# Four feed-forward blocks in seven half-width products per 2x2 set of tiles, with the conditioning rows moved ahead of them

## Chip, cores and metric

One core of one Trainium2 chip. The metric is the device time of one launch in microseconds (us). The profile is of one execution on the chip.

## What is computed

The reference runs two transformer blocks over 512 tokens of width 1024 in fp32. What matters here (cut):

```python
def _conv_ffn(h, w_up, conv_w, w_down):
    u = causal_depthwise_conv(h @ w_up, conv_w)
    a, b = jnp.split(u, 2, axis=-1)
    return (jax.nn.silu(a) * b) @ w_down

def swiglu(h, w_gu, w_down):
    g, u = jnp.split(h @ w_gu, 2, axis=-1)
    return (jax.nn.silu(g) * u) @ w_down

c_act = jax.nn.silu(c)
for i in range(2):
    mod = c_act @ mod_w[i] + mod_b[i]          # 9 vectors of 1024: shift, scale, gate, three times
    sh0, sc0, g0, sh1, sc1, g1, sh2, sc2, g2 = jnp.split(mod, 9, axis=-1)
    x = x + 0.5 * g0 * swiglu(modulate(rms_norm(x, norm_g[i, 0]), sh0, sc0), ffn_w_gu[i, 0], ffn_w_down[i, 0])
    x = x + g1 * mixer(modulate(rms_norm(x, norm_g[i, 1]), sh1, sc1))   # pooling, then differential attention
    x = x + 0.5 * g2 * swiglu(modulate(rms_norm(x, norm_g[i, 2]), sh2, sc2), ffn_w_gu[i, 1], ffn_w_down[i, 1])
```

`_conv_ffn` stands once, in the block ahead of this loop, and `swiglu` four times. Each has 1024 inputs, 2 x 2816 hidden columns and 1024 outputs.

## The kernel before

Activations lie transposed, features on the 128 partitions and 512 tokens along the free axis. A product in fp32 is made of three in the rounded type fp32r: a value is split into a high part (rounded) and a low part (the rest), and `product` (L1924 to L1926) issues high weight by high activation, high by low, and low by high, each 128x128 by 512 columns, into one PSUM bank. A weight unit is one output tile of 128 features: SP loads it into one of the four slots of `stage`, ACT writes its high part (`hi`, L655), DVE its low part (`lo`, L1144), each into one of two buffers, and PE waits for DVE.

The program runs in this order: the input products of the first mixer (`mix_in`), its merge and its output product (`mix_out`), feed-forward block 0 with the convolution (`up0`, `down0`), block 1, the pooling mixer, blocks 2 and 3, the attention, and block 4. Ahead of each stands a normalisation, in which PE spreads the scale over the partitions (`spread_rstd`, L1960), ACT and DVE round and split the normalised rows, and POOL makes half of the low parts (L564). In a feed-forward block `up` takes 44 units of 24 matmuls (22 pairs of a gate tile and an up tile) and `down` 8 outputs of 22 hidden tiles each, in three units; the pairs run in a loop of two. Of each pair ACT takes the silu of the gate (L715), DVE the product (L1234), and ACT and DVE split it (L718, L1241). In block 0 DVE also applies the taps of the convolution (L1216 to L1221).

The 144 conditioning rows (`mod`, L1185) are on DVE: each multiplies a 512 KB slice of `mod_w` by the activated condition and sums it. Slices come by POOL's queue (L536) into two buffers. 25 stand in `mix_in`, 32 in the merge, 7 in `mix_out`, 21 in `down0`, 44 in `up1` and 15 in `down1`.

Each engine runs its own list in the order in which the program is written; what holds an instruction back is the semaphores named at its wait. The change touches `plan_stream`, the loading on SP, `mod_loads` on POOL, and `up`, `down` and `mod` on each engine.

## Time and profile before

| | us |
|---|---|
| median of 3 runs | 2854.73 (2853.56 to 2866.36) |
| span of the profiled execution | 2868.0 |
| PE, ACT, DVE, POOL busy in it | 2783.2, 979.6, 1428.6, 241.9 |
| from one normalisation's spread to the next, feed-forward block 2 | 369.6 |
| the same, feed-forward block 3 | 369.1 |

The span is the profiled execution's own time, from its first instruction to its last. PE is busy in 97% of it. A row of a timeline begins with the start and the length; in brackets stand the idle time of that engine before the row and what ended it. PE rows overlap (a matmul's record is longer than the distance to the next), so the pace of PE is read from one start to another.

### The profile page before, as it was taken

The page shows a single profiled execution, that of the slowest core. Times are in us where ns is not written, and L with a number is a line of the kernel's source. Part 1 is how long each engine was busy: PE and PEld are TensorE (multiplying, and loading weights), DVE is VectorE, ACT ScalarE, POOL GpSimd, SP SyncE. Part 2 cuts the span into 40 slices and gives each one's busy share as a digit, 9 for nine tenths or more (in the row PEclk, how much of TensorE's full clock was granted, in tenths as well). Part 3 has the DMA queues.
Part 4 walks back from the last instruction along what each step waited for, and adds up shares of the span by engine and source line. Part 5 has one row for each costly group of instructions (what it writes and reads, how often), then busy time and mean ns, then how long its engine had stood idle before and what let it go on. Part 6 is the DMA issues. An engine that isn't in the chain of part 4 may idle for free.

```text
span 2868.0 us, 40754 instructions
## 1 busy us (share of the span) xinstructions
PE 2783.2 (97%) x16211; PEld 2249.2 (78%) x16211; DVE 1428.6 (50%) x2059; ACT 979.6 (34%) x1530; POOL 241.9 (8%) x318
## 2 busy tenths in 40 slices
PE   8999888999999999999989999999999999999998
PEld 7855777887887878888878888788887866788887
DVE  4588643666776455555443332433324876433322
ACT  3355443333332232222342222322223265422222
POOL 1000110112000111001110000100002300100000
PEclk8899999999999999999999999999999999999999
DMA  6331001673332655566323333233333310233332
GB/s 234 115 99 59 3 3 32 218 229 118 102 93 87 204 152 195 186 199 197 100 68 95 95 95 98 88 95 95 92 101 97 108 37 23 77 100 95 93 94 70
DMA packets 89844, 311.07 MB, mean 108 GB/s; under 512 B 11632, under 2 KB 12400, under 8 KB 89584
## 3 DMA queue, kind: packets, MB, share of 16 engines
q1 hardware_dynamic: 66928, 232.62, 26.0%
q0 software_dynamic: 22784, 76.56, 8.7%
q8 instruction: 98, 1.61, 0.2%
q14 instruction: 34, 0.28, 0.0%
HBM read 305.99 MB, written 2.10 MB: 107 GB/s over the span
## 4 chain that ended last, share of the span: by engine, by line
PE 91%; DVE 4%; ACT 3%; issue 1%; POOL 1%; DMA 1%; SPq 0%; DVEq 0%; ACTq 0%; POOLq 0%
PE psum L1924 24%; PE psum L1926 24%; PE psum L1925 24%; PE psum L2101 1%; PE psum L2103 1%; PE psum L2102 1%; PE psum L2612 1%; PE psum L2601 1%; PE psum L1999 1%; PE psum L1995 1%; PE psum L1996 1%; PE psum L2303 1%; PE psum L2076 1%; PE psum L2392 1%; PE psum L2273 1%
## 5 line engine op out<-in xcount | busy, mean ns | idle before, releaser
L1144 DVE TENSOR_TENSOR w_lo<-stage,w_hi 128x1024 fp32r<-128x1024 f32 (+2 forms) x441 | 518.3, 1175 | 827.4 <-ACT w_hi L655 827.2
L655 ACT ACTIVATE w_hi<-stage 128x1024 fp32r<-128x1024 f32 (+2 forms) x441 | 449.7, 1020 | 1206.1 <-PE psum L1926 1171.7
L1924 PE MATMUL psum<-h_hi,w_hi 128*128 128x512 f32 (+1 forms) x2024 | 792.7, 392 | 3.3 <-DVE w_lo L1144 2.3
L1925 PE MATMUL psum<-h_lo,w_hi 128*128 128x512 f32 (+1 forms) x2024 | 790.9, 391 | 0.0
L1926 PE MATMUL psum<-h_hi,w_lo 128*128 128x512 f32 (+1 forms) x2024 | 790.5, 391 | 0.0
L1924 PEld LDWEIGHTS psum<-h_hi,w_hi 128*128 128x128 f32 (+1 forms) x2024 | 381.1, 188 | 86.7 <-DVE w_lo L1144 4.4
L1926 PEld LDWEIGHTS psum<-h_hi,w_lo 128*128 128x128 f32 (+1 forms) x2024 | 381.0, 188 | 80.2
L1925 PEld LDWEIGHTS psum<-h_lo,w_hi 128*128 128x128 f32 (+1 forms) x2024 | 381.1, 188 | 79.6
L1924 PE MATMUL psum<-hid_hi,w_hi 128*128 128x512 f32 x880 | 344.0, 391 | 6.5 <-DVE hid L1234 6.5
L1926 PE MATMUL psum<-hid_hi,w_lo 128*128 128x512 f32 x880 | 343.4, 390 | 0.0
L1925 PE MATMUL psum<-hid_lo,w_hi 128*128 128x512 f32 x880 | 343.2, 390 | 0.0
L1924 PEld LDWEIGHTS psum<-hid_hi,w_hi 128*128 128x128 f32 x880 | 165.7, 188 | 42.9 <-DVE hid L1234 8.6
L1234 DVE TENSOR_TENSOR hid<-s_buf,psum 128x512 f32<-128x512 f32 x88 | 60.5, 687 | 266.5 <-PE psum L1926 264.9
L1926 PEld LDWEIGHTS psum<-hid_hi,w_lo 128*128 128x128 f32 x880 | 165.6, 188 | 34.5
L1925 PEld LDWEIGHTS psum<-hid_lo,w_hi 128*128 128x128 f32 x880 | 165.7, 188 | 34.2
L1185 DVE CUSTOM_DVE_ANT_0 mod_w<-mod_w,c_act 128x1024 f32<-128x1024 f32 x144 | 175.3, 1217 | 0.1
L536 POOL DMA_DIRECT2D mod_w<-in_mod_w x144 | 76.9, 534 | 1036.5 <-DVE modv L1185 859.2
L718 ACT ACTIVATE hid_hi<-hid 128x512 f32 (+1 forms) x110 | 68.0, 618 | 54.8 <-DVE hid L1234 54.8
L666 ACT ACTIVATE norm_t<-xT 128x512 f32<-128x512 f32 x64 | 40.2, 630 | 128.2 <-DVE xT L1258 121.2
L557 POOL TENSOR_TENSOR rexp<-norm_t 128x512 f32<-128x512 f32 x8 | 10.3, 1286 | 820.5 <-ACT norm_t L666 820.5
L1241 DVE TENSOR_TENSOR hid_lo<-hid,hid_hi 128x512 f32 (+1 forms) x110 | 75.2, 683 | 0.0
L557 POOL TENSOR_TENSOR rexp<-rexp,norm_t 128x512 f32<-128x512 f32 x40 | 51.4, 1285 | 270.5 <-ACT norm_t L666 269.9
(440 smaller groups left out, 3023.0 us busy)
## 6 DMA issues: line engine op xcount, KB each, us to landing
stage<-in_up SPq DMA_DIRECT2D x220, 512.0 KB, 3.6
mod_w<-in_mod_w POOLq DMA_DIRECT2D x144, 512.0 KB, 4.3
stage<-in_down SPq DMA_DIRECT2D x80, 448.0 KB, 3.3
stage<-in_down SPq DMA_DIRECT2D x40, 512.0 KB, 3.5
stage<-in_w_in SPq DMA_DIRECT2D x24, 512.0 KB, 3.6
stage<-in_w_qkv SPq DMA_DIRECT2D x24, 512.0 KB, 3.6
stage<-in_w_merge SPq DMA_DIRECT2D x16, 512.0 KB, 4.5
turned_n<-in_cmp_w SPq DMA_DIRECT2D x1, 4096.0 KB, 13.1
```

What stands on the lines that cost most here:

```text
L536: pool.dma_start(mod_w[:, slot], A["mod_w"][bass.ds(t, 1)].rearrange("a p n -> (a p) n")).then_inc(mod_in[slot], 16)
L557: pool.tensor_tensor(sq_sum, sq(n_norm, 0) if k == 1 else sq_sum, sq(n_norm, k), ALU.add).then_inc(acc_done, 1)
L655: act.activation(w_hi[:, c % 2, 0:kt * cols], stage[:, c % NSTAGE, 0:kt * cols], ACT.Copy).then_inc(hi_done, 1)
L666: act.activation(sq(n_norm, k), xT[:, k], ACT.Square).then_inc(sq_done, 1)
L718: act.activation(hid_hi[:, bass.ds(2 * i + q, 1), :].rearrange("p a n -> p (a n)"), hid[:, q], ACT.Copy).then_inc(hidhi_done, 1)
L1144: dve.tensor_tensor(w_lo[:, c % 2, 0:kt * cols], stage[:, c % NSTAGE, 0:kt * cols], w_hi[:, c % 2, 0:kt * cols].bitcast(F32), ALU.subtract ...
L1185: dve.tensor_tensor_reduce(out=mod_w[:, t % 2], in0=mod_w[:, t % 2], in1=c_act[:], scale=1.0, scalar=0.0, op0=ALU.mult, op1=ALU.add, accum ...
L1234: dve.tensor_tensor(hid[:, q], s_buf[:, q], taps[:, 1] if f == 0 else bank(s.tile + 2 * q + 1), ALU.mult).then_inc(hid_done, 1)
L1241: dve.tensor_tensor(hid_lo[:, tile, :].rearrange("p a n -> p (a n)"), hid[:, q], hid_hi[:, tile, :].rearrange("p a n -> p (a n)").bitcast( ...
L1924: pe.matmul(dst, wh[:, n], a_hi[:, k], start=start and n == 0, stop=False)
L1925: pe.matmul(dst, wh[:, n], a_lo[:, k], start=False, stop=False)
L1926: m = pe.matmul(dst, wl[:, n], a_hi[:, k], start=False, stop=stop and n == kt - 1)
```

## The change

**Feed-forward blocks 1 to 4.** The first four units (two gate tiles, two up tiles) stay as they were (`first_units` and two more, with 512 columns). All else is taken in sets of two by two: two output tiles, input tiles in pairs, and two halves of the tokens. Such a set, called a group, is made of seven products `P1` to `P7` of half width (256 columns) in place of eight. Ten groups `g` (two gate tiles each) alternate with ten groups `u` (two up tiles each); each takes the place of two units, has four pairs of inputs, and 12 matmuls in a product. For the outputs the pairs of hidden tiles are taken in two rounds of four, with four groups `d` (two output tiles each) in a round, and the last three pairs in six groups of one to three (`CLOSING`): 34 groups with 124 pairs in all, listed in `GROUPS`.

The products need sums and differences of weights and of activations. Five parts of weights are split for each group: `a` and `b` (1024 wide, two pieces each), `s4`, `s2` and `q` (512 wide). Three of the weight sums are made by DMAs that add into SBUF, issued by POOL (`sum_s1`, `sum_s3`, `sum_s4`), one on DVE (`sum_s2`). The split buffers are single: a part of the next group is written when the product that read the last one is done. The sums of the normalised rows are made on POOL (`hsum`), their differences on DVE. Products come together in PSUM: ACT copies intermediate states out (`snap`), DVE adds (`row1`, `c22`), and PE goes on in the same bank once a copy was made. Hidden pieces are kept in seven forms (the four quarters but one, and four combinations), which ACT and DVE split as 1792 columns at once.

PE runs `P1` and `P5` of a group, then `P3` of the one before, `P6`, `P4` of the one before, `P2` and `P7`.

**Conditioning rows.** All 144 stand ahead of block 1: 25 in `mix_in`, 40 in the merge, 14 in `mix_out`, 22 in `up0` (one a pair) and 43 in `down0`. The two buffers of `mod_w` and that of the condition then serve blocks 1 to 4.

The diff, cut:

```diff
+HALF = S // 2
+ROUNDS = [(0, 4), (4, 4)]
+CLOSING = [(8, 2, 1), (8, 2, 3), (8, 3, 0), (10, 1, 1), (8, 3, 2), (10, 1, 3)]
...
+ST_PE = in_turn(["P1", "P5", "P3", "P6", "P4", "P2", "P7"], ("P3", "P4"), ["P3", "P4"])
+ST_SPLIT = in_turn(["a", "s4", "s2", "q", "b"], ("s4", "q"), ["s4", "q"])
+PART_OF = {"P1": "a", "P5": "a", "P3": "s4", "P6": "s2", "P4": "q", "P2": "b", "P7": "b"}
...
-        MOD_AT = {"mix_in": 0, "merge": 25, "mix_out": 57, "down0": 64, "up1": 85, "down1": 129}
+        MOD_AT = {"mix_in": 0, "merge": 25, "mix_out": 65, "up0": 79, "down0": 101}
...
+            def sum_s1(f, G):
+                n, q = group_kp(G) * P, place[f, G, 0]
+                pool.wait_ge(loaded[q % NSTAGE], 16 * (q // NSTAGE + 1))
+                pool.dma_start(stage[:, q % NSTAGE, n:2 * n], group_source(f, G)[:, 4 * n:5 * n],
+                               accum_op=ALU.add).then_inc(st_s1_in[G % 2], 16)
...
+                for G in range(NG + 1):                      # ACT, per group
...
+                            snap("s1", G)
+                            snap("s5", G)
+                            part_hi("a", G + 1)
...
+                        silu("12", G - 1)
+                        part_hi("s4", G)
+                        snap("s6", G)
+                        part_hi("s2", G + 1)
...
+                        part_hi("q", G)
+                    if late == "u":
+                        hid_high(late_at)
+                        part_hi("b", G + 1)
+                    if kind == "g":
+                        silu("22", G)
...
                         lo(c + 2, i)
...
-                        if f == 1:
-                            mod(MOD_AT["up1"] + 2 * q, i)
+                        mod(MOD_AT["up0"] + q, i)
                         lo(c + 3, i)
...
-                        if s.name in MOD_AT and n < KD - 1:
-                            mod(MOD_AT[s.name] + 3 * n + j)
+                        if n < KD - 1:
+                            for t in range(43 * (3 * n + j) // 21, 43 * (3 * n + j + 1) // 21):
+                                mod(MOD_AT[s.name] + t)
...
+                for G in range(NG + 1):                      # DVE, per group
...
+                        sum_s2(G + 1)
+                        part_lo("a", G + 1)
+                        row1(G - 1)
...
+                        hid_dif(late_at)
+                        part_lo("s4", G)
...
+                        part_lo("s2", G + 1)
+                        hid21(G - 1)
+                        hid_dif4(late_at)
...
+                        part_lo("q", G)
+                        part_lo("b", G + 1)
+                    if late == "u":
+                        hid_low(late_at)
+                        c22(G)
...
+                def strassen(name, G):                       # PE
+                    kp = group_kp(G)
+                    pe.wait_ge(st_lo, split_of(f, PART_OF[name], G))
+                    bank_free(name, G)
...
+                    dst = gamma(G) if name in ("P5", "P3") else alpha(G) if name == "P2" else beta(G)
+                    start, stop = name in ("P1", "P5"), name in ("P4", "P3")
+                    for j in range(kp):
+                        w, low = wh[:, j * P:(j + 1) * P], wl[:, j * P:(j + 1) * P]
+                        pe.matmul(dst, w, operand(name, G, 0, j), start=start and j == 0, stop=False, skip_group_check=True)
+                        pe.matmul(dst, w, operand(name, G, 1, j), start=False, stop=False, skip_group_check=True)
+                        m = pe.matmul(dst, low, operand(name, G, 0, j), start=False, stop=stop and j == kp - 1,
+                                      skip_group_check=True)
+                    m.then_inc(st_prod, 1)
```

In `bank_free`, `P6` waits for the copy `s1` of its group, `P2` for `s5`, `P7` for `s6`, and `P4` for `c22`; `P1` and `P5` wait until the group two back has been taken out of their banks.

**Where instructions stand.** DVE at the start of the up part of block 1 before: the last low part of the normalised rows, then two units (`w_lo<-stage,w_hi` is the low part of a weight unit):

```order
L1172 SCALAR_TENSOR_TENSOR h_lo<-rexp,modv,h_hi 128x512 [waits hhi_done]
L1144 TENSOR_TENSOR w_lo<-stage,w_hi 128x1024 [waits hi_done]
L1234 TENSOR_TENSOR hid<-s_buf,psum 128x512 [waits unit_done,silu_done]
L1144 TENSOR_TENSOR w_lo<-stage,w_hi 128x1024 [waits hi_done]
L1241 TENSOR_TENSOR hid_lo<-hid,hid_hi 128x512 [waits hidhi_done]
```

and DVE after the change, while PE is at a gate group `g`. The rows are the low part of `a`, `row1` and the product of the pair before (L1728), the differences of its hidden pieces (L1760, L1763), low parts of `s4` and `s2`, the fourth quarter and its difference (L1751, L1771), low parts of `q` and `b`, the low part of the seven hidden pieces (L1777), and `c22` of `g` (L1735):

```order
L1672 TENSOR_TENSOR w_lo<-stage,w_hi 128x1024 [waits st_hi]
L1721 TENSOR_TENSOR c_act<-psum,c_act 128x512 [waits st_snap,st_prod]
L1728 TENSOR_TENSOR hraw<-c_act,rexp 128x512 [waits st_hlo,st_silu,st_row1]
L1760 TENSOR_TENSOR hraw<-hraw 128x512 [waits st_mult]
L1763 SCALAR_TENSOR_TENSOR hraw<-hraw 128x256 [waits st_ht]
L1672 TENSOR_TENSOR w_lo<-mod_w,w_hi 128x512 [waits st_hi] x2
L1751 SCALAR_TENSOR_TENSOR hraw<-psum,rexp 128x256 [waits st_silu,st_prod]
L1771 SCALAR_TENSOR_TENSOR hraw<-hraw 128x256 [waits st_hid21,st_ht]
L1672 TENSOR_TENSOR w_lo<-mod_w,w_hi 128x512 [waits st_hi]
L1672 TENSOR_TENSOR w_lo<-stage,w_hi 128x1024 [waits st_hi]
L1777 TENSOR_TENSOR hid_lo<-hraw,hid_hi 128x1792 [waits st_hhi]
L1735 TENSOR_TENSOR norm_t<-psum,norm_t 128x256 [waits st_snap,st_prod]
```

Where four instructions stood for two units, thirteen now stand for a group, which takes the place of two units. The matching rows of ACT after the change, from the high part of `a` on; the last but two is a silu, and the last two are the copies `s1` and `s5` of the up group `u`:

```order
L1027 ACTIVATE w_hi<-stage 128x1024 [waits st_prod,st_s1_in1,loaded3]
L1027 ACTIVATE w_hi<-mod_w 128x512 [waits st_prod,st_s4_in0]
L1040 ACTIVATE norm_t<-psum 128x256 [waits st_prod]
L1027 ACTIVATE w_hi<-mod_w 128x512 [waits st_prod,st_s2]
L1027 ACTIVATE w_hi<-mod_w 128x512 [waits st_prod,st_a22_0]
L1061 ACTIVATE hid_hi<-hraw 128x1792 [waits st_ht]
L1027 ACTIVATE w_hi<-stage 128x1024 [waits st_prod,st_s3_in1,loaded0]
L1054 ACTIVATE norm_t<-norm_t 128x256 [waits st_c22]
L1040 ACTIVATE c_act<-psum 128x256 [waits st_prod,st_mult]
L1040 ACTIVATE c_act<-psum 128x256 [waits st_prod]
```

The copy `s1` of `u` stands behind the silu (L1054), which waits for DVE's `c22`, the last row of the fence before. Third, DVE in `up0` after the change; the rows of L1576 are new there, and before, L1626 was followed at once by the low part of the next unit:

```order
L1626 TENSOR_TENSOR hid<-s_buf,taps 128x512 [waits unit_done,silu_done,tap_done]
L1576 ISA mod_w,modv<-mod_w,c_act 128x1024 [waits mod_in1]
L1576 ISA modv 128x1
L1535 TENSOR_TENSOR w_lo<-stage,w_hi 128x1024 [waits hi_done]
L1632 TENSOR_TENSOR hid_lo<-hid,hid_hi 128x512 [waits hidhi_done]
```

A conditioning row now stands between the product of a pair and the low part of a unit, which PE waits for.

## Rows read from the trace of the kernel before

**Rows 1.** The page's busy times, shares and instruction counts by engine.

```profile
PE 2783.2 (97%) x16211; PEld 2249.2 (78%) x16211; DVE 1428.6 (50%) x2059; ACT 979.6 (34%) x1530; POOL 241.9 (8%) x318
```

**Rows 2.** Windows, block 2: length, busy PE, PEld, DVE, ACT, POOL; clock, DMA, GB/s.

```profile
1455.00:1824.00 369.00, 367.22 (x1622) 303.40 (x1621) 124.09 (x136) 107.70 (x136) 12.90 (x10) 1.00 0.31 93
```

**Rows 3.** Chain of waits, the spreads at both ends of block 2: start, length, what.

```profile
1455.02 1.72 PE psum L1960 x8
...
1824.65 1.17 PE psum L1960 x8
```

**Rows 4.** Timeline of PE in `up2`, first matmuls of units four apart.

```profile
1498.95 0.39 PE L1924 MATMUL psum<-h_hi,w_hi 128*128 128x512 f32 x1
...
1520.71 0.39 PE L1924 MATMUL psum<-h_hi,w_hi 128*128 128x512 f32 x1
```

**Rows 5.** Timeline of PE in the pooling mixer, 256-column matmuls 27 apart.

```profile
1424.68 0.28 PE L2526 MATMUL psum<-w_hi,h_hi 128*128 128x256 f32 x1
...
1427.90 0.28 PE L2526 MATMUL psum<-w_hi,h_hi 128*128 128x256 f32 x1
```

**Rows 6.** DVE by line and shape: busy, mean ns, idle before and its releaser.

```profile
L1144 DVE TENSOR_TENSOR w_lo<-stage,w_hi 128x1024 fp32r<-128x1024 f32 x340 | 416.1, 1224 | 528.3 <-ACT w_hi L655 528.2
...
L1241 DVE TENSOR_TENSOR hid_lo<-hid,hid_hi 128x512 f32 x90 | 61.5, 683 | 0.0
...
L1612 DVE TENSOR_TENSOR psum<-psum,tri 128x256 f32<-128x256 f32 x32 | 13.8, 430 | 18.6 <-PE psum L2303 18.5
```

**Rows 7.** ACT by line and shape, same columns.

```profile
L655 ACT ACTIVATE w_hi<-stage 128x1024 fp32r<-128x1024 f32 x340 | 360.7, 1061 | 967.5 <-PE psum L1926 934.6 <-PE psum L1999 27.6 <-PE psum L2496 2.0
...
L655 ACT ACTIVATE w_hi<-stage 128x512 fp32r<-128x512 f32 x20 | 12.5, 625 | 9.5 <-PE psum L1926 7.9 <-PE psum L2528 1.6
...
L970 ACT ACTIVATE X<-psum 128x256 f32<-128x256 f32 x40 | 15.2, 381 | 37.9 <-PE psum L2390 32.9 <-PE psum L2368 3.9
```

**Rows 8.** Timeline of ACT in `up2`, released by a unit's last matmul.

```profile
1499.15 1.06 ACT L655 ACTIVATE w_hi<-stage 128x1024 fp32r<-128x1024 f32 x1 [3.86 <-PE psum L1926]
```

**Rows 9.** Timeline of DVE in `up2`, two instructions that follow each other.

```profile
1505.69 1.23 DVE L1144 TENSOR_TENSOR w_lo<-stage,w_hi 128x1024 fp32r<-128x1024 f32 x1 [0.34 <-ACT w_hi L655]
1506.83 0.68 DVE L1241 TENSOR_TENSOR hid_lo<-hid,hid_hi 128x512 f32 x1
```

**Rows 10.** Timeline of PE, first matmuls after two short stops.

```profile
1420.95 0.40 PE L2526 MATMUL psum<-w_hi,h_hi 128*128 128x256 f32 x1 [2.62 <-POOL h_lo L564]
...
2445.19 0.80 PE L1924 MATMUL psum<-h_hi,w_hi 128*128 128x512 f32 x1 [1.78 <-DVE w_lo L1144]
```

**Rows 11.** Windows right behind those stops (columns of rows 2).

```profile
1421.00:1424.40 3.40, 3.40 (x17) 3.40 (x18) 3.10 (x5) 2.64 (x4) 1.52 (x2) 0.52 0.00 0
...
2445.00:2448.00 3.00, 2.81 (x7) 2.26 (x8) 1.36 (x3) 1.58 (x2) 0.00 (x0) 0.52 0.57 156
```

**Rows 12.** Timeline of POOL, the last low part ahead of block 2.

```profile
1466.52 1.29 POOL L564 TENSOR_TENSOR h_lo<-rexp,h_hi 128x512 fp32r<-128x512 f32 x1 [0.90 <-ACT h_hi L699]
```

**Rows 13.** The page's costliest groups, an addition of two 128x512 tiles on POOL.

```profile
L557 POOL TENSOR_TENSOR rexp<-rexp,norm_t 128x512 f32<-128x512 f32 x40 | 51.4, 1285 | 270.5 <-ACT norm_t L666 269.9
```

**Rows 14.** Timeline of DVE in `up0`, second taps of a pair and the next unit's low part.

```profile
766.25 0.75 DVE L1216 TENSOR_SCALAR taps<-psum,vec 128x512 f32<-128x512 f32 x1 [0.81 <-PE psum L1926]
...
769.59 1.22 DVE L1144 TENSOR_TENSOR w_lo<-stage,w_hi 128x1024 fp32r<-128x1024 f32 x1
```

**Rows 15.** Chain of waits in the merge, a conditioning row, its buffer's next load, the next row.

```profile
621.18 1.22 DVE mod_w L1185
...
623.05 5.08 DMA mod_w<-in_mod_w
628.16 1.22 DVE mod_w L1185
```

**Rows 16.** The page's DMA queues: packets, MB, share of 16 engines' span.

```profile
q1 hardware_dynamic: 66928, 232.62, 26.0%
```

**Rows 17.** The page's DMA issues: KB each, median us from issue to landing.

```profile
mod_w<-in_mod_w POOLq DMA_DIRECT2D x144, 512.0 KB, 4.3
```

713 lines of the change are left out of this document (603 added, 110 removed).

## Prediction

> **What bounds the kernel now.** I read the page's busy times first: PE is busy in 2783.2 of 2868.0 us [rows 1]. Then the windows, to see whether that holds where the change works: in feed-forward block 2 PE is busy in 367.2 of 369.0 us at full clock, DVE in 124.1 and ACT in 107.7 [rows 2]. The chain of waits dates the block from one spread to the next, 1455.02 to 1824.65, 369.6 us [rows 3]. Blocks 1 to 4 are alike. So a block's time is its matmuls: four units of 24 take 1498.95 to 1520.71, 21.76 us for 96, or 0.2267 us each [rows 4]. ACT and DVE idle for two thirds of a block; the reader should see that this slack is an average, and that a unit's weights are split a whole unit ahead.
>
> The profiled execution, 2868.0 us, is 13.3 us longer than the median of runs, 2854.73. The sum is made against 2868.0; I take 13 off at the end. What a measurement can tell from no change is about 0.5%, 14 us.
>
> **Matmuls: a gain.** Per block 62 units with 1488 matmuls of 512 columns go, 337.3 us at 0.2267. In their place come 124 pairs x 7 x 3 = 2604 of 256 columns. The nearest rows are the pooling mixer's fp32r matmuls of 256 columns, each with a weight load of its own as here: 27 steps in 3.22 us, 0.1193 us each [rows 5]. That makes 310.7 us, **26.7 us less** per block, 107 in four. A product of 12 is 1.43 us, a group 10.02, a pair of groups (g, u) 20.04 where 21.76 was.
>
> The Trainium skill's page "TensorE: Matmul & The Clock Gate" (section on the back-to-back issue gap) would give N/2.4 + 2.5 ns, 216 and 109 ns; by it a block saves 36.6 us, all four 40 us more, and the forecast would be about 2996. The rows [rows 4, 5] show 10 ns more per matmul at both widths, and I keep the rows.
>
> **A pair of groups: a new wait.** The question is whether ACT and DVE, which run their lists in order, follow PE in 20 us. Their durations: a split of 1024 columns takes 1.22 on DVE and 1.06 on ACT, of 512 0.68 and 0.63, a PSUM operation of 256 columns 0.43 and 0.38 [rows 6, 7]. The 1792-column split has no row; by the slope from 512 to 1024 columns (1.06 ns a column on DVE, 0.85 on ACT) I estimate 2.03 and 1.71, nearest to the 1024 row; the ends are two 1024-splits (2.45, 2.12) and the slope alone (1.9, 1.5). ACT starts 0.20 after the last matmul it waits for (1499.15 after 1498.95) [rows 4, 8]; instructions on one engine overlap by 0.09 (1.23 long, 1.14 apart) [rows 9].
>
> From P1 of g at 0, as the order fences list it. ACT copies s1 at 1.63 and s5 at 3.07, and splits `a` for u, 3.36 to 4.42. DVE takes `a` low to 5.68, row1 to 6.28, the product of the pair before to 7.0, its two differences to 8.17, s4 and s2 low to 9.35, the last quarter and its difference to 10.15, q low to 10.74. ACT meanwhile can split the seven hidden pieces only when the last difference is there: 10.18 to 11.90. Behind it stands `b` for u, to 12.86. DVE: `b` low to 14.12, the low part of the hidden pieces to 16.06, c22 of g to 16.40. ACT: the silu on c22 to 16.84, then the copy s1 of u, 16.75 to 17.13. PE's P6 of u waits for that copy. It is due after one group and three products, at 14.3, and starts at 17.2: **PE idles 2.8 us**, once in each pair. All links are data or queue order between ACT and DVE; none shortens because an average is low. The u half has slack: DVE holds 6.7 us of work there, 10.8 in the g half. P7 of u loses 0.4 more behind the copy s6, so the pair takes 23.25 us at full clock.
>
> The clock comes on top. After idling 2.62 us PE was granted 0.52 of full clock (near its lower level of 1.2 GHz, of 2.4) for the next 3.4 us, and after 1.78 us 0.52 for 3.0 us [rows 10, 11]. A stop of 2.8 us lies above both. At half clock 3.3 us do the work of 1.7; the loss is partly taken from the wait that follows, and the walk gives **24.45 us**, 4.4 more than PE's work. Nine pairs of a block meet the wait: 39.6 us. Bounds: no stop, 0; and 6 us a pair, if the 1792-column splits cost like two of 1024 and the cross-engine waits 0.1 more each.
>
> **Start of a block.** The four plain units stay. The normalised rows' sums are new on POOL: the last low part there ends at 1467.81, 12.8 after the spread [rows 3, 12], then come eight additions of 128x512 at 1.285 [rows 13]. Seven end at +21.8, a little later for two DMA issues ahead of them; DVE's difference and the low part of the fourth unit follow to 25.5, where PE wanted it at 22.3. So 3.2 us. The first `a` comes 1.7 late, and P6 of the first group 5.7, since the split of the first hidden pieces stands on ACT ahead of the first copy. 10.6 us, with two more for the clock: **12.6**. Bounds 5 and 18.
>
> **Closing groups.** Products of 3 to 9 matmuls give 30.1 us of PE work, but the splits and the additions to x keep DVE 31 to 37 us: **8** us, bounds 0 and 14. The eight full groups for outputs keep PE's pace: each has 7 DVE splits and sums and 6 additions, about 8.5 us of 10.
>
> **Per block** -26.7 + 39.6 + 12.6 + 8 = **+33.5**, in four **+134**.
>
> **Conditioning rows.** Removed from block 1, where PE hid them: nothing gained. New places: `up0`, one in each pair ahead of the next unit's low part. There DVE's second taps begin at 766.25, and that low part ends at 770.81 [rows 14]; the unit's slot is at 766.05 + 5.44 = 771.49, slack 0.68 us. A row costs 1.14, so PE stops 0.5 per pair: with 0.1 for restarts, 22 x 0.6 = **13** us. In `down0` 43 rows stand in 21 slots of about 4.99 us (22 matmuls). With two buffers, a row, the issue, the load and the row again take 621.18 to 628.16, 6.98 us for two rows [rows 15]; with the median load of 4.3 instead of 5.08 [rows 17], 6.2 to 6.4. 21 x 1.4 = **28** us (13 to 41). In the merge and `mix_out` fifteen rows more: **6** (0 to 13). Together **+47**, bounds 25 and 70; a slot that gives PE a stop of a microsecond can also cost clock, which is the upper end.
>
> **Bytes.** A block reads 124 x 8 blocks of 65.5 KB, 65.0 MB where it read 32.5; 24.4 MB of it are added into SBUF. The queue of loads moved 232.6 MB in 26.0% of the span, 312 GB/s while busy [rows 16], so a block has 130 us of plain transfers and 78 more if an adding transfer costs the same. No row has one; bounds are 1 times a plain one (it moves no less) and 3 times (a read of the source, a read and a write of the destination), 208 to 365 us of about 400. I take it as hidden.
>
> **Sum.** 134 + 47 = +181: 3049 against 2868.0, **3036** against the median. The range of this case: 2985 to 3085, by the bounds on the wait and the rows.
>
> **Rivals.**
> 1. Lighter stops (0.22). The clock stays up after 2.8 us: nine pairs lose 3.2 each, start and closing 15.6, so a block -26.7 + 28.8 + 15.6 = +17.7, four 71 us; rows at their lower bound, 25: **2951**. For it: ACT's real waits could be shorter by a few handoffs, and stops then stay under those of rows 10. Against it: [rows 11] shows both short stops followed by half clock.
> 2. PE stays the bound (0.14), and the kernel is **faster**. Decides: the chain from P1 of g to the copy of u must fit. Of its 17.2 us the part after q low is the 1792-split, `b`, hidden low, c22 and silu; with PE due at 14.34 it must lose 2.8 us, a fifth of the 14 us in which DVE and ACT work. Then -107, with 20 for starts and closings and 25 for rows: **2793**. For it: 50% idle ACT and DVE. Against: each duration is a row, and the order is fixed.
> 3. Adding transfers bind (0.10). At three times a plain one a block's transfers take 365 us, and some 50 pass at its start and end in which only the four slots can be filled ahead; `s1`, `s3`, `s4` land late: a landing of more than about 8 us (4.3 for a 512 KB load) stops the split of `a`, thus P1. A block then takes some 415 us, four 182 more, with 47 for rows **3084**. By the Trainium skill's "DMA: Bandwidth & Descriptors" (rules for kernel authors) an accumulating DMA reads its destination and writes it later; that speaks for more than the plain price, and no run here shows how much.
> 4. Gain and stops cancel (0.09), within 0.5%: stops of 1 us a pair and 10 us at start and end, so a block -7.7, against 31 for the rows: about **2855**, 2840 to 2869.
>
> My forecast has 0.45. The range of 2850 to 3110 leaves out most of rival 2 and the upper tail of 3, less than 0.2. Faster 0.14 (rival 2), same 0.09 (rival 4), slower 0.77 (forecast and rivals 1 and 3).
>
> **What to look for.** Busy PE falls from 97% to under 90%. The three lines of 256-column matmuls run at 0.119 us. PE idles 2.5 to 3 us ahead of P6 of each u, released by ACT's copy of s1, with a granted clock near 0.5 behind it; a pair of groups takes 24.4 us, a block about 403. In `up0` and `down0` PE waits for DVE's low parts. DMA bytes rise by 130 MB to about 440. I am wrong if P6 starts without idling (rival 2), if the stops leave the clock at 1.0 (rival 1), or if DMA waits lead the idle time (rival 3).

## The result, and the profile after

The changed kernel takes 3222.95 us (median of 4 runs, 3216.45 to 3227.45), the kernel before in the same session 2854.14: a ratio of 1.128 with a 95% interval of 1.124 to 1.131. It is slower, as forecast, but by 369 us, not by 181, and it lies outside the range of 2850 to 3110. The profiled execution spans 3220.5 us, 352.5 more than the one before (2868.0).

The page's first part after the change (for before: [rows 1]):

```profile
PE 2826.8 (88%) x20675; PEld 2483.1 (77%) x20675; DVE 2140.2 (66%) x3253; ACT 1318.6 (41%) x2206; POOL 639.8 (20%) x758
```

The windows from one normalisation's spread to the next: block 0, then blocks 1 to 4 (columns as in [rows 2]).

```profile
691.10:1121.00 429.90, 391.65 (x1624) 310.12 (x1623) 298.51 (x420) 111.51 (x134) 46.40 (x73) 0.96 0.47 157
1121.00:1554.40 433.40, 366.38 (x2737) 354.55 (x2738) 299.03 (x433) 191.81 (x306) 112.25 (x120) 0.92 0.67 156
...
1594.50:2037.50 443.00, 374.95 (x2739) 362.84 (x2739) 299.51 (x431) 194.03 (x307) 112.30 (x120) 0.90 0.66 153
2037.50:2478.10 440.60, 369.68 (x2739) 357.69 (x2738) 299.60 (x432) 193.42 (x306) 112.25 (x120) 0.91 0.66 154
...
2769.70:3202.20 432.50, 365.76 (x2738) 353.19 (x2738) 297.08 (x430) 191.78 (x304) 112.23 (x120) 0.92 0.65 150
```

The spread ahead of block 0 came at 673.0 before and at 691.1 now, and block 0 took 373.3 us before: the stages with moved rows lost 18.1 + 56.6 = 74.7 us. Blocks 1 to 4 took 368.9, 370.1, 369.1 and 368.8 before; they lost 64.5, 72.9, 71.5 and 63.7, together 272.6. The other stages make up the last 5. The reader should see the clock in the window rows: PE's busy time in blocks 1 to 4, 367 to 368 us before, is 366 to 375 us now, although a block's matmuls are 27 us less at full clock. At 0.90 to 0.92 of the clock they take longer.

**Where PE stops in block 2.** The timeline of PE, with the idle time ahead of a row and what ended it:

```profile
1620.77 0.80 PE L2520 MATMUL psum<-h_hi,w_hi 128*128 128x512 f32 x1 [8.64 <-DVE w_lo L1535]
...
1678.82 0.36 PE L2670 MATMUL psum<-dif_hi,w_hi 128*128 128x256 f32 x1 [3.02 <-issue]
...
1702.01 0.55 PE L2670 MATMUL psum<-dif_hi,w_hi 128*128 128x256 f32 x1 [3.00 <-issue]
...
1726.67 0.55 PE L2670 MATMUL psum<-hid_hi,w_hi 128*128 128x256 f32 x1 [6.20 <-DVE hid_lo L1777]
...
1797.75 0.55 PE L2670 MATMUL psum<-dif_hi,w_hi 128*128 128x256 f32 x1 [3.00 <-issue]
...
1823.36 0.36 PE L2670 MATMUL psum<-dif_hi,w_hi 128*128 128x256 f32 x1 [3.00 <-issue]
...
1847.81 0.35 PE L2670 MATMUL psum<-dif_hi,w_hi 128*128 128x256 f32 x1 [3.02 <-issue]
...
1989.42 0.55 PE L2670 MATMUL psum<-hid_hi,w_hi 128*128 128x256 f32 x1 [3.88 <-issue]
...
2031.85 0.80 PE L2535 MATMUL psum<-cst,rexp 128*128 128x1 f32 x3 [4.99 <-POOL rexp L779]
```

The stops of 3.0 us are those ahead of P6 that the prediction walked to (2.8); "issue" only says that the view finds no releaser for a wait on ACT's copies. What ended it is seen on DVE and on ACT just ahead of 1702.01:

```profile
1698.84 2.02 DVE L1777 TENSOR_TENSOR hid_lo<-hraw,hid_hi 128x1792 fp32r<-128x1792 f32 x1
1700.77 0.42 DVE L1735 TENSOR_TENSOR rexp<-psum,rexp 128x256 f32<-128x256 f32 x1
```

```profile
1701.22 0.42 ACT L1054 ACTIVATE rexp<-rexp 128x256 f32<-128x256 f32 x1 [3.56 <-DVE rexp L1735]
1701.55 0.64 ACT L1040 ACTIVATE c_act<-psum 128x256 f32<-128x256 f32 x2
```

The 1792-column low part (2.02, estimate 2.03), c22, the silu, the copy: the queue order of the prediction, link by link. From stop to stop a pair takes 23.19 us at full clock (1678.82 to 1702.01; forecast 23.25) and 24.45 us (1823.36 to 1847.81) to 25.61 us (1797.75 to 1823.36) with half clock (forecast 24.45). The windows behind stops, in order of time; the first one stands at a block's start and the last at its end, and the second follows the stop at 1678.82:

```profile
1616.10:1626.20 10.10, 5.43 (x13) 4.27 (x14) 10.10 (x8) 2.12 (x2) 4.21 (x4) 0.50 0.38 114
1679.00:1701.00 22.00, 19.97 (x168) 19.60 (x167) 16.01 (x22) 11.06 (x17) 5.28 (x6) 1.00 0.79 181
1702.00:1708.60 6.60, 6.59 (x32) 6.60 (x33) 3.37 (x5) 3.97 (x8) 2.37 (x3) 0.53 0.70 120
1726.60:1732.60 6.00, 5.93 (x30) 5.96 (x31) 1.18 (x4) 0.77 (x2) 1.75 (x2) 0.54 0.78 150
1797.70:1804.00 6.30, 6.25 (x30) 6.28 (x31) 3.21 (x4) 3.87 (x8) 2.03 (x3) 0.52 0.65 131
1824.30:1827.60 3.30, 3.30 (x18) 3.30 (x17) 1.88 (x3) 1.41 (x4) 0.88 (x1) 0.50 0.76 107
2029.10:2037.50 8.40, 5.65 (x21) 5.26 (x22) 1.08 (x3) 1.47 (x4) 1.26 (x1) 0.50 0.43 153
```

Half clock is near the lower of the two levels, 1.2 GHz of 2.4. Behind the stops at 1702.01 and 1797.75 it lasted 6 us and more. Behind the one at 1823.36 it lasted some 3.3 us, which is what the prediction took from [rows 11], and behind the equally long one at 1678.82 the clock stayed up. The short stretch is the usual one: of the 28 stops of 2.6 to 3.4 us ahead of `dif` products in the pairs of blocks 1 to 4, 21 were followed by 2.8 to 3.4 us of half clock, three by about 6, and four by none. So the prediction's price for these stops was fair. It set two us a block for half clock at all other stops, and there is more of it ahead of the output groups (1726.60), at a block's start (1616.10) and at its end (2029.10).

**Block 2 in three parts.** DVE's `row1` dates the first and the last group of `up` in every kernel (L1541 marks the block's ends):

```profile
1594.52 0.18 DVE L1541 RECIPROCAL rstd<-std 128x4 f32<-128x4 f32 x1 [11.12 <-ACT std L953]
...
1657.83 0.68 DVE L1721 TENSOR_TENSOR rexp<-psum,rexp 128x512 f32<-128x512 f32 x1
...
1979.10 0.68 DVE L1721 TENSOR_TENSOR c_act<-psum,c_act 128x512 f32<-128x512 f32 x1
...
2037.53 0.18 DVE L1541 RECIPROCAL rstd<-std 128x4 f32<-128x4 f32 x1 [7.35 <-ACT std L953]
```

PE's own work in them, at the paces of [rows 4, 5]: start 39.5 (27.8 to the end of the four plain units, the eight products up to `P3` of the first group, 0.2), middle 27 groups of 10.02 or 270.5, end 32.9 (what is left of 369.6 - 26.7 = 342.9). So the start cost 63.3 - 39.5 = 24, the middle 321.3 - 270.5 = 51, the end 58.4 - 32.9 = 25, and 100 - 26.7 is the loss of 73. Of the three, 16, 36 and 16 us are stops of PE over 0.25 us; the other 8, 15 and 10 are for the most part half clock. Block 2 is the slowest: on the mean of blocks 1 to 4 the stops are 68 us and the rest 27. The same table for all kernels (us, one profile each; the stages ahead of block 0 vary by up to 16 us between profiles of equal code, so block 0 is the place to read the rows):

| kernel | ratio to before (95%) | block 0 | start | middle | end | block 2 |
|---|---|---|---|---|---|---|
| before | 1 | 373.3 | | | | 370.1 |
| changed | 1.128 (1.124 to 1.131) | 429.9 | 63.3 | 321.3 | 58.4 | 443.0 |
| e1 rows alone | 1.024 (1.020 to 1.028) | 431.9 | | | | |
| e2 sums on DVE | 1.113 (1.108 to 1.118) | 432.3 | 52.5 | 316.3 | 57.7 | 426.5 |
| e3 c22 early | 1.099 (1.094 to 1.103) | 435.4 | 62.5 | 303.7 | 59.5 | 425.7 |
| e4 plain transfers | 1.115 (1.110 to 1.119) | 435.4 | 62.6 | 314.5 | 56.4 | 433.5 |
| e5 stops filled | 1.103 (1.099 to 1.108) | 432.3 | 58.5 | 311.1 | 58.2 | 427.8 |
| e6 queue orders | 1.073 (1.068 to 1.079) | 435.8 | 48.1 | 298.5 | 57.5 | 404.1 |
| e7 row between taps | 1.021 (1.016 to 1.027) | 417.6 | | | | |
| e8 closing order | 1.125 (1.121 to 1.129) | 434.1 | 62.7 | 319.7 | 56.7 | 439.1 |
| e9 hidden first | 1.074 (1.069 to 1.078) | 434.3 | 48.1 | 295.6 | 60.5 | 404.2 |
| e10 two rows in up0 | 1.009 (1.006 to 1.012) | 386.1 | | | | |
| e11 idle additions | 1.000 (0.998 to 1.002) | | | | | |
| e12 adds first | 1.122 (1.117 to 1.127) | 431.6 | 56.9 | 322.3 | 58.7 | 437.9 |
| e13 square sums late | 1.129 (1.126 to 1.133) | 433.6 | 63.3 | 321.1 | 56.6 | 440.9 |
| e14 all together | 1.055 (1.052 to 1.059) | 390.0 | 48.1 | 297.2 | 56.7 | 402.0 |

The medians of before were 2865 us beside e1 to e8, 2860 beside e9 to e11 and 2858 beside e12 to e14, so the ratios compare, not the times. One per cent is 29 us. Where an experiment is said to take so much less than the change, that is the difference of two ratios, good to some 15 us. One of the four executions of e6 was a slow one of 6205 us, and the ratio leaves it out.

### The profile page after: what moved, and what is told of

The parts are those of the page before. It is cut to its first block, busy times and chain, and to the rows that moved or that the text cites. A ratio compares the mean times of both kernels' runs of the same rounds, so it can differ in the third digit from the quotient of the medians.

```text
span 3220.5 us, 52371 instructions
## 1 busy us (share of the span) xinstructions
PE 2826.8 (88%) x20675; PEld 2483.1 (77%) x20675; DVE 2140.2 (66%) x3253; ACT 1318.6 (41%) x2206; POOL 639.8 (20%) x758
## 4 chain that ended last, share of the span: by engine, by line
PE 64%; DVE 13%; issue 8%; DMA 8%; ACT 5%; POOL 1%; DVEq 0%; POOLq 0%; ACTq 0%; SPq 0%
PE psum L2670 12%; PE psum L2671 11%; PE psum L2672 11%; DMA mod_w<-in_mod_w 5%; PE psum L2520 4%; PE psum L2521 4%; PE psum L2522 4%; DVE w_lo L1535 3%; DVE mod_w L1576 2%; DMA mod_w<-in_down 2%; DVE w_lo L1672 1%; ACT w_hi L1027 1%; PE psum L2768 1%; PE psum L2770 1%; PE psum L2769 1%
## 5 line engine op out<-in xcount | busy, mean ns | idle before, releaser
L1672 DVE TENSOR_TENSOR w_lo<-stage,w_hi 128x1024 fp32r<-128x1024 f32 (+3 forms) x272 | 307.3, 1130 | 336.9 <-ACT w_hi L1027 336.1
L2670 PE MATMUL psum<-hid_hi,w_hi 128*128 128x256 f32 x1232 | 367.8, 299 | 99.8 <-DVE hid_lo L1777 49.6
L2670 PE MATMUL psum<-h_hi,w_hi 128*128 128x256 f32 x1280 | 373.4, 292 | 10.0 <-DVE w_lo L1672 9.9
L2671 PE MATMUL psum<-h_lo,w_hi 128*128 128x256 f32 x1280 | 369.2, 288 | 0.0
L2672 PE MATMUL psum<-h_hi,w_lo 128*128 128x256 f32 x1280 | 368.2, 288 | 0.0
L2671 PE MATMUL psum<-hid_lo,w_hi 128*128 128x256 f32 x1232 | 360.9, 293 | 0.0
L2672 PE MATMUL psum<-hid_hi,w_lo 128*128 128x256 f32 x1232 | 360.5, 293 | 0.0
L2520 PE MATMUL psum<-h_hi,w_hi 128*128 128x512 f32 (+1 forms) x744 | 300.5, 404 | 51.4 <-DVE w_lo L1535 50.5
L1535 DVE TENSOR_TENSOR w_lo<-stage,w_hi 128x1024 fp32r<-128x1024 f32 (+2 forms) x185 | 253.3, 1371 | 126.9 <-ACT w_hi L925 121.9
L2521 PE MATMUL psum<-h_lo,w_hi 128*128 128x512 f32 (+1 forms) x744 | 295.9, 398 | 0.0
L2522 PE MATMUL psum<-h_hi,w_lo 128*128 128x512 f32 (+1 forms) x744 | 295.3, 397 | 0.0
```

Of the source, the lines that this page charges most:

```text
L1535: dve.tensor_tensor(w_lo[:, c % 2, 0:kt * cols], stage[:, place[c] % NSTAGE, 0:kt * cols], w_hi[:, c % 2, 0:kt * cols].bitcast(F32), ALU.s ...
L1672: dve.tensor_tensor(w_part(1, name, kp), raw_part(f, name, G), w_part(0, name, kp).bitcast(F32), ALU.subtract).then_inc(st_lo, 1)
L2520: pe.matmul(dst, wh[:, n], a_hi[:, k], start=start and n == 0, stop=False)
L2521: pe.matmul(dst, wh[:, n], a_lo[:, k], start=False, stop=False)
L2522: m = pe.matmul(dst, wl[:, n], a_hi[:, k], start=False, stop=stop and n == kt - 1)
L2670: pe.matmul(dst, w, operand(name, G, 0, j), start=start and j == 0, stop=False, skip_group_check=True)
```

## The experiments

The edits are cut to the lines that matter; loads, loops and waits that follow from them are left out.

**e1: the rows alone.** The kernel before with the rows' places of the change.

```diff
-        MOD_AT = {"mix_in": 0, "merge": 25, "mix_out": 57, "down0": 64, "up1": 85, "down1": 129}
+        MOD_AT = {"mix_in": 0, "merge": 25, "mix_out": 65, "up0": 79, "down0": 101}
```

> The kernel before with nothing but the conditioning rows moved as in the change (25, 40, 14, 22 and 43 of them; feed-forward blocks 1 to 4 untouched). Theory A (the rows themselves cost what block 0 and the stages ahead of it lost in the change, 75 us): 2915 to 2940 us. Rival (the rows cost the 47 us of the prediction, and the other 28 come from elsewhere in the change): 2890 to 2905 us.

Measured: 2933.26, 2.4% or 70 us over before, 58.6 of it in block 0 as in the change (56.6). The rows are an independent loss, and nothing of the seven-product groups is in it.

**e2: POOL's sums moved to DVE.** At the start of a block, DVE and POOL of the changed kernel:

```profile
1610.59 10.12 DVE L1535 TENSOR_TENSOR w_lo<-stage,w_hi 128x1024 fp32r<-128x1024 f32 x1 [4.20 <-ACT w_hi L925]
```

```profile
1607.99 0.87 POOL L843 DMA_DIRECT2D stage<-in_up  x1
1608.58 1.20 POOL L850 DMA_DIRECT2D stage<-in_up  x1
1609.14 10.48 POOL L870 TENSOR_TENSOR hsum<-h_hi,h_lo 128x512 f32<-128x512 f32 x8
```

A subtraction of 1.2 us took 10.1, until POOL's eight additions were over, and PE stopped about 8.6 us for it, in all four blocks.

```diff
-                    pool.tensor_tensor(hsum[:, k], h_hi[:, k].bitcast(F32), h_lo[:, k].bitcast(F32), ALU.add).then_inc(st_sum, 1)
+                    dve.tensor_tensor(hsum[:, k], h_hi[:, k].bitcast(F32), h_lo[:, k].bitcast(F32), ALU.add).then_inc(st_sum, 1)
```

> The changed kernel with the eight sums of the normalised rows made by DVE in place of POOL, four ahead of the fourth plain unit's low part and four behind it. Theory A (DVE's low part takes 10.1 us in place of 1.2 because POOL's eight additions run beside it, and PE then stops 8.6 us, once a block): the low part takes 1.2 us again and the kernel 3180 to 3200 us. Rival (that low part was held by something else, the transfers of the first groups for one): it stays above 5 us and the time within 10 us of 3223.

Measured: 3181.73; the low parts of the plain units take 1.2 us again, the stop is gone, the start 10.8 us shorter in block 2, 1.5% or 42 us in all. The Trainium skill's "SBUF — State Buffer" (who interferes with whom) says that a DVE instruction with two SBUF inputs contends with a GpSimd instruction that reads SBUF, the second to issue being blocked until the first is over; the trace agrees that they contend, and shows DVE held for seven additions, not one. e11 and e12 come back to it.

**e3: c22 early.**

```diff
+                    if kind in ("g", "u"):
+                        c22(G)
+                    if kind == "u":
+                        hid22(G)
                     if G + 1 < NG:
                         part_lo("b", G + 1)
                     if late == "u":
                         hid_low(late_at)
-                    if kind in ("g", "u"):
-                        c22(G)
-                    if kind == "u":
-                        hid22(G)
```

> The changed kernel with two DVE operations (c22 and, in up groups, hid22) ahead of the next group's low part of b and of the 1792-column low part, in place of behind them. Theory A (the 3 us stop ahead of P6 of u is queue order: copy s1 behind a silu behind c22 behind the 1792-column split): seven stops a block go with their share of the clock, 3095 to 3140 us. Rival (ACT and DVE are too slow for a pair whatever their order, so the stop moves to the next wait): above 3180 us, with PE waiting for low parts or copies elsewhere in the pair.

Measured: 3148.41, 8 us above the expected range and below the rival's; by the ratios it is 2.9% or 83 us less than the change. The 3.0 us stops and their half clock are gone, so their cause was the order. But a stop of 1.46 us took their place, as the rival has it: on PE, and on ACT ahead of it,

```profile
1695.77 0.36 PE L2670 MATMUL psum<-dif_hi,w_hi 128*128 128x256 f32 x1 [1.46 <-issue]
```

```profile
1694.25 0.63 ACT L1048 ACTIVATE rexp<-rexp 128x512 f32<-128x512 f32 x1 [3.77 <-DVE rexp L1721]
1694.79 0.61 ACT L1027 ACTIVATE w_hi<-mod_w 128x512 fp32r<-128x512 f32 x1
1695.31 0.36 ACT L1040 ACTIVATE c_act<-psum 128x256 f32<-128x256 f32 x1
```

P7 of u now waits for the copy s6 behind a silu that DVE releases late. A pair takes 21.4 us (1790.58 to 1811.97), where the plain units took 21.76: even with the stop halved, the pair gives back nearly all of its 1.72 us.

**e4: plain transfers.** `accum_op=ALU.add` left out at L843, L850 and L857; the weight sums s1, s3 and s4 are left out by that.

> The changed kernel with its adding transfers made plain ones of the same size from the same queue; the sums s1, s3 and s4 of weights are left out by that. Theory A (stops in the up part are queue order; only the closing groups wait for landings): 3190 to 3215 us. Rival B (the doubled traffic and the adding transfers hold the blocks): below 3120 us.

Measured: 3189.2, 1.3% or 38 us less, at the edge of theory A and far from what rival B asks. The 3.0 us stops stay. The end of block 2 is only 2.0 us shorter, so it isn't shown that the closing groups are the ones that wait for landings. The page's DMA part gives the price of adding; POOL's queue (q0) in the changed kernel and in e4:

```profile
q0 software_dynamic: 81536, 174.11, 28.0%
```

```profile
q0 software_dynamic: 53120, 174.11, 18.7%
```

Before, POOL's queue moved 76.56 MB in 8.7% of 2868 us. The 97.6 MB more took 28.0% of 3220.5 less that, 652 us of all engines, or 150 GB/s. As plain transfers the same bytes took 18.7% of 3190.7 less that, 347 us or 281 GB/s. So adding costs 1.9 times a plain transfer of the same size (2.05 times the rows' larger loads, which ran at 307 GB/s), inside the bounds of 1 and 3. A block's transfers then take at most 130 + 2.05 x 78 = 290 us of 440. They are hidden but for late landings, and what those cost is at most the 38 us that e4 got back, good to some 15.

**e5: the stops filled**, so that the clock has no stop to fall behind.

```diff
+                fill = {("P6", GROUPS.index(("u", p))): 6 for p in (2, 3, 5, 6, 7, 9, 10)}
+                fill.update({("P1", GROUPS.index(("d", (p0, 4, 0)))): 13 for p0 in (0, 4)})
+                fill.update({("P1", 0): 5, ("P6", 0): 8})
...
+                    for _ in range(count):
+                        pe.matmul(psum[:, 5, 0:256], ident, cst[:, 0:256], start=True, stop=True)
```

> The changed kernel with idle matmuls on PE ahead of the waits at which it stops: 6 ahead of P6 of seven u groups of a block, 13 ahead of the two rounds of output groups, 17, 5 and 8 at a block's start (about 0.43 us each, a little less than the stops last; results go to an unused bank). Theory A (about 34 us a block are matmuls run at half clock behind the stops): the granted clock in blocks 1 to 4 rises above 0.97 and the kernel takes 3120 to 3165 us. Rival (what runs slowly behind a stop is waited for by nobody, since ACT and DVE are behind anyway): the clock rises and the time stays within 20 us of 3223.

Measured: 3158.61, 2.4% or 70 us less, with the same waits and more matmuls. The mean granted clock, changed kernel and e5:

```profile
core 0: 3220.5 us, clock 0.932
```

```profile
core 0: 3155.8 us, clock 0.973
```

So at least 17 us a block were half clock. The account of block 2 gives more: 100 us over PE's own work, less 67.5 of stops (those over 0.25 us, summed), leaves 33.

**e6: five queue orders together**: e2, e3, and

```diff
+                    if G < NG and kind != "d":
+                        snap("s6", G)
                     if late == "g":
                         silu("12", G - 1)
...
-                    if G < NG and kind != "d":
-                        snap("s6", G)
...
-                hid_high(0)
...
-                    if late == "u":
+                    if late == "u" or G == 0:
                         hid_high(late_at)
...
+                    ahead = late == "u" and G + 1 < NG and GROUPS[G + 1][0] == "d"
+                    if ahead:
+                        hid_low(late_at)
```

> The changed kernel with five orders changed: sums of normalised rows on DVE, c22 and hid22 early (both as tried apart), the copy s6 on ACT ahead of the silu and of the high part of s4, the first pair's hidden pieces split behind the first copies, and the low part of the hidden pieces ahead of b where output groups follow. Theory A (PE's stops are places in the queues): to what the two changes gave apart (-42 and -83 us) come 1.5 us for each of seven pairs, 4 to 6 us at a block's start and 2 to 4 us for each round of output groups: 2985 to 3040 us. Rival (ACT and DVE have no more room, stops move on): above 3060 us.

Measured: 3077.28, 5.4% or 155 us less than the change; above the expected 2985 to 3040, and on the rival's side. Blocks take 398 to 408 us. The start is down to 48.1, but the stops ahead of output groups stayed (6.5 and 7.1 us in block 2), and PE now waits at each P1, for ACT's or DVE's last quarter two groups back. PE and ACT of e6:

```profile
1665.38 0.55 PE L2667 MATMUL psum<-hid_hi,w_hi 128*128 128x256 f32 x1 [6.53 <-DVE hid_lo L1768]
```

```profile
1658.62 1.67 ACT L1020 ACTIVATE w_hi<-mod_w 128x512 fp32r<-128x512 f32 x3 [3.58 <-DMA mod_w<-in_up]
```

With PE faster, ACT waits 3.6 us for an adding transfer (s4), and everything behind it in its queue is late.

**e7 and e10: the rows in other places**, on the kernel of e1. First one row between the taps of a pair in `up0`, then two rows there and one a slot in `down0`.

```diff
                             tap(0, c, i)
+                            mod(MOD_AT["up0"] + q, i)
                             tap(1, c + 1, i)
...
-                            mod(MOD_AT["up0"] + q, i)
                         lo(c + 3, i)
```

```diff
-        MOD_AT = {"mix_in": 0, "merge": 25, "mix_out": 65, "up0": 79, "down0": 101}
+        MOD_AT = {"mix_in": 0, "merge": 25, "mix_out": 65, "up0": 79, "down0": 123}
...
+                            mod(MOD_AT["up0"] + 2 * q + 1, i)
```

> The kernel before with the rows moved as in the change, but in up0 each row stands between the two taps of its pair, where DVE was seen idle for 1.1 to 1.6 us. Theory A (0.8 us a pair are lost because the row stands ahead of a low part that PE waits for): 14 to 20 us below the rows alone. Rival (the rows cost by their transfers or by DVE time): within 6 us of the rows alone.

> The kernel before with the rows moved, 44 of them in up0 (one between the taps of a pair, one behind its low parts) and 21 in down0 (one a slot), in place of 22 and 43. Theory A (down0 loses 39 us because two buffers give two rows only every 6 to 7 us, where a slot of 5 us wants two): down0 takes about 125 us again, and the kernel 25 to 40 us less than with one row between the taps (2923): 2883 to 2900. Rival (each row outside its old place costs DVE time, wherever): above 2912.

Measured: e7 2923.24, 10 us below e1, between theory A and the rival, and the intervals of the two ratios overlap. Its block 0 is 14.3 us below e1 (431.9 to 417.6), all of it in `up0`, where PE's matmuls now span 243.0 us in place of 257.4 (241.9 before); that is theory A's sum, in one profile. e10 is at 2886.21, as theory A has it, with block 0 at 386.1 and the ratio down from 1.021 to 1.009; `down0` spans 121.1 us in place of the 162.5 of e7 (121.2 before). In the changed kernel DVE shows both mechanisms: in `up0` the row ahead of the low part (PE then stops 0.51 us, and a pair takes 11.70 us in place of 10.88), in `down0` rows that wait for their buffer's load.

```profile
770.78 1.22 DVE L1576 CUSTOM_DVE_ANT_0 mod_w<-mod_w,c_act 128x1024 f32<-128x1024 f32 x1
...
771.93 1.22 DVE L1535 TENSOR_TENSOR w_lo<-stage,w_hi 128x1024 fp32r<-128x1024 f32 x1
...
1000.11 1.23 DVE L1576 CUSTOM_DVE_ANT_0 mod_w<-mod_w,c_act 128x1024 f32<-128x1024 f32 x1 [1.95 <-DMA mod_w<-in_mod_w]
```

**e8 and e13: the end of a block.** Another order of the closing groups, and POOL's square sums one group later.

```diff
-CLOSING = [(8, 2, 1), (8, 2, 3), (8, 3, 0), (10, 1, 1), (8, 3, 2), (10, 1, 3)]
+CLOSING = [(8, 2, 2), (8, 2, 3), (8, 3, 0), (8, 3, 1), (10, 1, 2), (10, 1, 3)]
```

```diff
-                    if G >= NG - 3:
+                    if G >= NG - 2:
                         for k in range(2):
-                            gather(n_norm + 1, 2 * (G - NG + 3) + k)
-                gather(n_norm + 1, 6)
+                            gather(n_norm + 1, 2 * (G - NG + 2) + k)
+                for k in range(4, 7):
+                    gather(n_norm + 1, k)
```

> The changed kernel with the six closing groups in another order: outputs 2 and 3 first with two pairs, then outputs 0 and 1 with three, then 2 and 3 with the last one, so that no group of one pair is followed by one of three. Theory A (a closing group waits for its own transfers, 5 us of landing against 2.5 us of work in a group of one pair, and these now land under the longer groups ahead): 15 to 35 us less than 3223. Rival (the closing groups are held by DVE's and ACT's work): within 10 us.

> The changed kernel with POOL's square sums for the next normalisation one closing group later in its queue, so that two adding transfers for s4 no longer stand behind them. Theory A (these transfers, late by 2 to 4 us each, set the closing groups): a block's end 5 to 10 us shorter, the kernel 20 to 40 us less than 3223. Rival (the closing groups are held by the splits and additions of ACT and DVE, and by half clock): within 12 us.

Measured: 3222.48 and 3229.08, both the same as the change; the end is 1.7 and 1.8 us shorter. Both times the rival held. What sets the end as a whole is not settled, but neither run moved one piece of it that the trace of the changed kernel shows. DVE splits the next stage's first two weight units (L1535) ahead of the block's last two additions to x (L1703):

```profile
2026.42 2.70 DVE L1535 TENSOR_TENSOR w_lo<-stage,w_hi 128x1024 fp32r<-128x1024 f32 x2 [0.26 <-ACT w_hi L925]
2029.05 0.74 DVE L1703 SCALAR_TENSOR_TENSOR xT<-psum,gates,xT 128x512 f32<-128x512 f32 x1
```

PE's last stop, the 4.99 us at 2031.85, waits for the square sums made from these additions. Behind block 4 no such units stand, and its last stop is shorter:

```profile
3198.12 1.05 PE L2535 MATMUL psum<-cst,rexp 128*128 128x1 f32 x8 [2.02 <-POOL rexp L779]
```

Block 4's end takes 52.2 us, those of blocks 1 to 3 take 56.5 to 59.2. No run tried the other order.

**e9: hidden pieces first**, on e6: on DVE the last quarter and its difference ahead of s4 and s2, and on ACT

```diff
+                    if late == "u":
+                        hid_high(late_at)
                     if G < NG:
                         part_hi("s4", G)
```

> The kernel with five queue orders changed (3077 us), and one more: the last quarter of the hidden pieces and its difference on DVE, and the high part of the seven pieces on ACT, stand ahead of the parts s4 and s2, the one of which waits for an adding transfer; where output groups follow, the low part of the seven pieces stands ahead of s4 too. Theory A (the 6.5 to 7.1 us stops ahead of the two rounds of output groups are this chain, behind a late transfer): they fall to 2 to 3 us, without half clock behind them, and the kernel takes 3015 to 3045 us. Rival (the chain is bound elsewhere): the stops stay above 5 us and the time above 3060.

Measured: 3075.06, no gain, though the stops fell as theory A said (to 2.8 to 2.9 us in all four blocks). PE of e9 shows where the time went:

```profile
1641.79 0.36 PE L2669 MATMUL psum<-h_hi,w_hi 128*128 128x256 f32 x1 [2.68 <-ACT norm_t L1044]
```

`P1` now waits up to 2.7 us for ACT's last silu in block 2, and the end grew by 3.0 us. What one wait gave, the next ones took.

**e11 and e12: what held DVE's subtraction.** Idle additions in the kernel before, and in the changed kernel POOL's sums ahead of its first two adding transfers.

```diff
+                if n_norm < 6:
+                    idle_adds(n_norm)
```

```diff
-                sum_s1(f, 0)
-                sum_s3(f, 0)
...
-                sum_s1(f, 1)
-                sum_s3(f, 1)
+                for G in range(2):
+                    sum_s1(f, G)
+                    sum_s3(f, G)
```

> The kernel before with nothing changed but eight idle additions of 128x512 on POOL at the start of feed-forward blocks 2 and 3, where the change has them (results go to a free buffer). Theory A (POOL's additions, one behind the other, hold a DVE subtraction that reads two SBUF tiles): the low part of the third unit takes about 10 us in place of 1.2 in these two blocks, PE stops some 8 us in each, and the kernel takes 15 to 25 us more than before. Rival (the long low part had another cause): the low part stays below 2 us and the time within 5 us.

> The changed kernel with POOL's eight sums of normalised rows ahead of the first two adding transfers that POOL issues, in place of behind them. Theory A (DVE's subtraction is held by the sums only where POOL has just issued adding transfers): the low part of the third unit takes under 3 us, as beside the idle additions alone (2.3), and the kernel 20 to 40 us less than 3223. Rival (the sums hold it wherever they stand): it stays at about 10 us less what runs ahead of it, and the time within 12 us.

Measured: e11 2858.35, no change; DVE's subtraction and POOL's additions there,

```profile
1455.47 2.28 DVE L1159 TENSOR_TENSOR w_lo<-stage,w_hi 128x1024 fp32r<-128x1024 f32 x1 [4.20 <-ACT w_hi L670]
```

```profile
1452.89 12.45 POOL L582 TENSOR_TENSOR mod_w<-h_hi,h_lo 128x512 f32<-128x512 f32 x8
```

so the additions alone cost it 1.1 us, less than one of them takes, and theory A of e2 fell in the form in which it was put. e12 3212.47, with the subtraction at

```profile
1612.88 2.34 DVE L1534 TENSOR_TENSOR w_lo<-stage,w_hi 128x1024 fp32r<-128x1024 f32 x1 [4.20 <-ACT w_hi L924]
```

as expected, and the start 6.4 us shorter. The ratio is 0.6% or 17 us lower, below the expected 20 to 40, and its interval overlaps with the change's, so a gain in time isn't shown. The additions hold DVE's subtraction for their whole length only where POOL has issued two transfers right ahead of them. That these transfers add does not matter: in e4 they are plain, and DVE and POOL show the same.

```profile
1601.72 9.53 DVE L1532 TENSOR_TENSOR w_lo<-stage,w_hi 128x1024 fp32r<-128x1024 f32 x1 [4.19 <-ACT w_hi L922]
```

```profile
1599.11 0.55 POOL L843 DMA_DIRECT2D stage<-in_up  x1
1599.66 0.54 POOL L849 DMA_DIRECT2D stage<-in_up  x1
1600.21 9.95 POOL L867 TENSOR_TENSOR hsum<-h_hi,h_lo 128x512 f32<-128x512 f32 x8
```

Why is open.

**e14: all together** (e6, the rows of e10, e13, and 13 idle matmuls ahead of the two rounds of output groups, 6 ahead of the first product).

> All that helped: the five queue orders (3077 us), the rows with two to a pair in up0 and 21 in down0, the square sums one group later, and idle matmuls ahead of the two rounds of output groups (13) and of a block's first product (6). Theory A (the causes add up): 45 to 55 us less for the rows, 10 to 30 for the square sums, 10 to 25 for the clock, so 2975 to 3010 us; that is still slower than before. Rival (they overlap): above 3020 us.

Measured: 3016.48, between the expected sum (up to 3010) and the rival's (above 3020). The rows' part arrived (block 0 at 390.0); of the rest, blocks 1 and 4 gained 10 us and blocks 2 and 3 2 to 7. It is 5.5% (5.2 to 5.9) slower than before, so no version here beats it.

## Why the prediction was right or wrong

The direction and the mechanism of the pair stood: the stop ahead of P6 (3.0 us, 2.8 forecast), its place in the queues, the period at full clock, the pace of the matmuls (0.119 us), and transfers at about twice the plain price that stay hidden but for some 38 us. Rivals 2 and 4 fell with it, rival 3 with e4, and rival 1 by the windows, where the clock fell behind most stops. The size was off. The forecast and block 2 beside each other (us; the 8 for the closing groups was not divided):

| | stops of PE | half clock and the rest | together |
|---|---|---|---|
| start | 10.6, measured 16 | 2, measured 8 | 12.6, measured 24 |
| middle | 28.8, measured 36 | 10.8, measured 15 | 39.6, measured 51 |
| end | | | 8, measured 25 (16 and 10) |
| block | | | 60.2, measured 100 |

The middle's 28.8 is nine times the 3.2 us of stops in the walk, and its 10.8 nine times 1.2. The steps that failed:

- **Half clock was priced at the pairs and hardly anywhere else.** The terms held 9 x 1.2 + 2 = 13 us a block for it; it cost some 33 in block 2 and 27 on the mean of the four, and filling stops gave back some 17 a block. "At half clock 3.3 us do the work of 1.7" was fair for the pairs; 8 us at the start and 10 at the end, where 2 were taken, make up most of the difference.
- **"The eight full groups for outputs keep PE's pace"** failed. They do inside a round, but its first product waits for the low part of the last pair's hidden pieces, which the walk itself had ending at 16.06 us in a stretch in which that product was due at 10.02. I followed the chain to P6 and not to this second reader: 6.20 us, twice a block, about 12. It was luck that two of the nine pair stops fell away (seven of some 3 us were seen), which hid about 6 us of it.
- **The start of a block**, forecast 12.6, cost 24. Some 8 of the missing 11 us are the subtraction held beside POOL's sums: the walk had 3.2 us for this wait, and e2 took 10.8 off the start by removing it. I had counted POOL's time and not what it does to DVE.
- **Closing groups**, forecast 8, cost 25. Stops of 16 us in all were seen, the last of 5 us for POOL's square sums; the rest is for the most part half clock. e4, e8 and e13 each left 56 us and more standing, so neither the price of adding, nor the order of groups, nor the place of the square sums is the cause alone. About 3 of the 5 us go with the next stage's two splits on DVE, by the contrast with block 4. What is left is the chain through ACT, DVE and short products; that was argued, not shown.
- **The rows**, forecast 47 with bounds of 25 and 70, cost 75 in the profile. `up0` lost 0.82 us a pair where 0.6 was taken, and `down0` 39 where 28 was taken (21 x 1.4 is 29.4), near its upper end of 41; both mechanisms were as forecast (e7, e10). The stages ahead lost 2 to 18 in profiles of the same code, against 6; the kernel before itself has profiles 13 us apart there (e11), so that part of the 75 is not measured well. e1 has 70 us for the rows in the whole time, 58 to 81 by its interval.

For the profile: 352.5 against 181, made of +139 for the blocks, +28 for the rows, and 5 in stages without a change (rounded).

## What to carry to other kernels

Matmul time that is saved is worth only what the other engines' chains leave of it: here 1.72 us a pair, and in e3 and e6 the pair took 21.4 us because waits of about one us followed each other through two in-order queues. Every stop of PE must be priced with the slow clock around it, those at the ends of a stage too, and not only the one that the walk looked for. And a walk through the queues has to be taken to every reader of each buffer, above all to the first one of the next stage.
